# A decoder trunk on one NeuronCore: another order of the chunk steps in the token mixer

## What is computed

```
m = w_out( [retention heads | HGRN2 heads | sliding-window attention] (x @ w_in) )
x = layernorm(alpha * x + m)
x = layernorm(alpha * x + w_down(relu(w_up(x))^2))
```

## Time and profile before

| | |
|---|---|
| median of 3 runs | 2735.28 us (2732.26 to 2736.43) |
| the profiled execution, its own time | 2732.12 us |
| its span, first to last instruction | 2730.3 us |
| TensorE busy | 2555.8 us, 94% of the span |
| VectorE, GpSimd, ScalarE busy | 1680.6, 997.7 and 836.7 us |
| mean granted TensorE clock | 0.973 |

### The profile page before, as it was taken

The page is one execution under the profiler, slowest core; times in us unless marked ns, Lnnn a source line. Parts: engine busy times, 40 slices in busy tenths (PEclk is TensorE's granted clock), DMA queues, the critical chain, the costliest instruction groups (busy, mean ns, idle before and its releaser), DMA issues. The chain is left out here.

```text
span 2730.3 us, 45275 instructions
## 1 busy us (share of the span) xinstructions
PE 2555.8 (94%) x18126; PEld 2366.2 (87%) x18126; DVE 1680.6 (62%) x3361; ACT 836.7 (31%) x1667; POOL 997.7 (37%) x1052
## 2 busy tenths in 40 slices
PE   7999988789999999999899999887999999999996
PEld 7998866588999999999899987666989999999996
DVE  3136678558855666666851367884596555666668
ACT  3235665232322221111122455661322222111110
POOL 0027666531555531122000466664325555222220
PEclk9999999789999999999999999997999999999998
DMA  4442232162233253223343531321622233432323
GB/s 168 148 157 88 90 108 54 34 197 82 80 108 113 95 181 94 92 93 95 109 146 130 166 105 57 106 69 40 196 76 95 95 123 116 158 95 91 94 79 112
DMA packets 225889, 295.83 MB, mean 108 GB/s; under 512 B 28817, under 2 KB 177617, under 8 KB 225649
## 3 DMA queue, kind: packets, MB, share of 16 engines
q1 hardware_dynamic: 225680, 292.94, 33.5%
HBM read 217.27 MB, written 77.66 MB: 108 GB/s over the span
## 5 line engine op out<-in xcount | busy, mean ns | idle before, releaser
L1089 PE MATMUL ps<-hid_hi,wd_hi 128*128 128x256 f32 (+2 forms) x800 | 257.5, 322 | 12.7 <-DVE acc_b L2778 6.7
L1090 PE MATMUL ps<-hid_lo,wd_hi 128*128 128x256 f32 (+2 forms) x800 | 255.3, 319 | 0.0
L1089 PE MATMUL ps<-hid_hi,wdl_hi 128*128 128x256 f32 (+2 forms) x800 | 255.2, 319 | 0.0
L1090 PE MATMUL ps<-hid_lo,wdl_hi 128*128 128x256 f32 (+2 forms) x800 | 255.1, 319 | 0.0
L1091 PE MATMUL ps<-hid_hi,wd_lo 128*128 128x256 f32 (+2 forms) x800 | 255.1, 319 | 0.0
L1091 PE MATMUL ps<-hid_hi,wdl_lo 128*128 128x256 f32 (+2 forms) x800 | 254.8, 318 | 0.0
L2762 DVE TENSOR_TENSOR acc_a<-ps,acc_a 128x512 f32<-128x512 f32 x208 | 143.9, 692 | 152.3 <-PE ps L1091 152.3
L3077 POOL TENSOR_TENSOR wq_lo_S<-ws,wq_hi_S 128x512 fp32r<-128x512 f32 x104 | 199.1, 1923 | 104.3 <-ACT wq_hi_S L2087 104.3
L2762 DVE TENSOR_TENSOR acc_b<-ps,acc_b 128x256 f32<-128x256 f32 (+1 forms) x416 | 178.2, 439 | 74.2 <-PE ps L1091 69.2
L3055 POOL TENSOR_TENSOR wl_lo<-wl_raw,wl_hi 128x2048 fp32r<-128x2048 f32 x14 | 63.8, 4558 | 415.7 <-ACT wl_hi L1789 415.6
L1089 PE MATMUL ps<-wi_hi,u_hi 128*128 128x320 f32 x600 | 185.7, 309 | 2.1 <-DVE wi_lo L2273 2.1
(11 more groups left out here) (329 smaller groups left out, 7872.2 us busy)
## 6 DMA issues: line engine op xcount, KB each, us to landing
wd_raw<-in_w_down SPq DMA_DIRECT2D x32, 1024.0 KB, 4.9
wq_raw<-in_w_up SPq DMA_DIRECT2D x26, 1024.0 KB, 6.1
wl_raw<-in_w_in SPq DMA_DIRECT2D x20, 1024.0 KB, 5.1
wi_raw<-in_w_in SPq DMA_DIRECT2D x15, 1280.0 KB, 6.6
hidscr<-h SPq DMA_DIRECT2D x32, 544.0 KB, 7.9
out_y<-xn SPq DMA_DIRECT2D x32, 512.0 KB, 4.6
hidscr<-h SPq DMA_DIRECT2D x32, 512.0 KB, 7.1
hid_raw<-hidscr SPq DMA_DIRECT2D x32, 512.0 KB, 3.5
```

The costliest lines, as they stand in the source:

```text
L1089: nc.tensor.matmul(out, a_hi, b_hi, start=start, stop=False)
L1090: nc.tensor.matmul(out, a_hi, b_lo, start=False, stop=False)
```

## The change

No instruction of arithmetic is added or taken away. Five lists are put in another order.

1. ScalarE: `window_weights` is cut into `_a` and `_b`, and all of `gates_sigmoid(g)` stands between them. From step 4 on, `dense c` stands at the end of the step, behind `gates_log`, and in step 4 still ahead of `split_wo(l, 0)`.
2. TensorE: the gates' transposes stand between the transposes of waves A and B.
3. VectorE, `heads_merge`: `cat_h` ahead of the state updates. `gates_sigmoid` is cut after its clip, the rest is `gates_keys`, right behind it.
4. VectorE: `front_silu` moves from ahead of `front_levels` to behind `heads_rstd`; `heads_low` of a prompt chunk moves into the next step, behind `front_queries`.
5. GpSimd: the low parts of `OUT_AFTER` move from the end of a step to the next one, behind `values` and a wait for the next gates (`f1`).

```diff
@@ TensorE, mix_step
                         window_weights(f, h, "A")
-                        window_weights(f, h, "B")
                         if g:
                             gate_transposes(g, f, h)
+                        window_weights(f, h, "B")
@@ ScalarE
-                def window_weights(c):
+                def window_weights_a(c):
                     act.wait_ge(wpe.sem, wpe.at("TA", c.w))
                     copy(probT[:, 0]...).then_inc(wa.step("TA"), 1)
+
+                def window_weights_b(c):
                     act.wait_ge(wpe.sem, wpe.at("TB", c.w))
...
                         window_norm(f, "B")
-                        dense(step, "c")
-                        window_weights(f)
+                        if step < 4:
+                            dense(step, "c")
+                        window_weights_a(f)
                         if g:
                             gates_sigmoid(g)
+                        window_weights_b(f)
                         dense(step, "d")
...
                     if f and f.prompt and g:
                         gates_log(g)
+                    if f and f.prompt and step >= 4:
+                        dense(step, "c")
                     if step == 4:
                         split_wo(l, 0)
@@ VectorE, heads_merge
-                    if c.prompt:
-                        heads_states(c)
                     dve.wait_ge(md.sem, md.at("sr", c.n))
                     v.tensor_tensor(cat_h[0:rows, :], ...).then_inc(md.step("rh"), 1)
+                    if c.prompt:
+                        heads_states(c)
@@ VectorE, mix_step
+                    past = chunk_at(l, step - 2)
                     if f:
                         front_queries(f)
+                    if past:
+                        heads_low(past)
                     if h:
                         heads_keys(h)
...
                     if f:
-                        front_silu(f)
                         front_levels(f)
...
                     if h:
                         heads_rstd(h)
+                    if f:
+                        front_silu(f)
                     if f and f.prompt:
                         window_sums(f, "B")
...
                             gates_sigmoid(g)
+                            gates_keys(g)
                         window_low(f)
...
                     if h and not h.prompt:
                         decode_states_h(h)
-                    if h:
                         heads_low(h)
@@ GpSimd, mix_step
                     if f:
                         values(f, h)
+                    if step - 1 in OUT_AFTER:
+                        if f:
+                            pool.wait_ge(gc.sem, gc.at("f1", f.n))
+                        for out in OUT_AFTER[step - 1]:
+                            split_wo(l, out)
+                    if f:
...
                         gate_weights(f)
...
-                        for out in OUT_AFTER.get(step, ()):
-                            split_wo(l, out)
```

More of the change, by code:

```diff
@@ L2330, in gates_sigmoid, with gates_keys @@
                                     ALU.mult, ALU.min).then_inc(gc.step("clip"), 1)
+                def gates_keys(c):
+                    dve.wait_ge(gc.sem, gc.at("clip", c.n))
                     dve.wait_ge(gh.sem, gh.at("r", c.n))
@@ L2625, in mix @@
                 gates_sigmoid(chunk_at(l, 0))
+                gates_keys(chunk_at(l, 0))
                 v.memset(st_r[:], 0.0).then_inc(zd.step("r"), 1)
```

## The result

| | before | after |
|---|---|---|
| median of 4 runs | 2735.86 us (2732.26 to 2742.40) | 2777.69 us (2772.82 to 2783.93) |
| ratio, 95% interval | | 1.0143 (1.0122 to 1.0165) |
| span of the profiled execution | 2730.3 us | 2773.1 us |
| mean granted TensorE clock | 0.973 | 0.960 |

The account below looks back on a forecast made before the run. TensorE's work (2555.8 of 2730.3 us) plus its gaps was taken as the bound. Layer terms of 5.05 and 4.55 us gave 9.6, so 2732.1 became 2741.7 us, median 2744.9; range 2730 to 2751.

Parts of the forecast that it names:

- the change, which adds no work, can only move gaps: Whole kernel: time is TensorE's work, busy 2555.8 of 2730.3 us, plus gaps; only the gaps would change.
- `window_out` at TA+6.2: Steps 5 to 7: `window_out` starts 6.2 us after TA, the start of wave A's transposes, 1.35 us later than before.
- `window_low` follows `window_out` (1.95 us) and its high part (0.6 us): TA+8.85: Step 6: `window_low` starts 8.85 us after wave A's transposes start (TA), instead of 9.10; net -0.25 us.
- The wait that I named as a sign: Steps 5 to 7: TensorE's wait on ScalarE ahead of `window_out` would be near 2.5 us.
- the +0.2: Step lengths 5 to 6 and 6 to 7: each 0.2 us longer, bounds -1.2 to +0.9.
- The lock that the prediction weighed: VectorE's clip beside GpSimd's split: begun first, the clip would be free and each of two step lengths 0.6 us shorter.
- Step 1: 0, for `g_qe` is early and ScalarE then waits for a load of weights: Step 1 of the mixer: the reordered ScalarE copies cost 0 us.
- rival C: Late silu delays SyncE's `hb` loads and output weights queued behind; some 3 us more a layer, 2751 us; chance 0.12.
- Step 4 to 5: Late drains delay the first output weights, `s_kT` and `dense a1`: 3.35 us a layer, bounds 2.3 to 4.1.
- -0.25 and +0.2: Step 7 into 8: 0.25 us shorter; step 8: 0.2 us longer, silu standing ahead of the decode window on VectorE.
- A: Rival: late output weights cost little, 1 us at step 4 into 5; +5 us, 2740 us; chance 0.20.
- B: Rival, faster: VectorE's chain keeps its gains, 1.45 us off each of three lengths, steps 4 to 7; chance 0.16.

Follow-up runs that it names:

- Run 4: Changed kernel plus 20 throwaway identity transposes on TensorE ahead of `window_out` in each of the 8 prompt steps; ratio 1.0106 to the kernel before.
- run 6: Kernel before with ScalarE's gate functions between its copies of waves A and B, plus 16 throwaway TensorE transposes ahead of `window_out`; ratio 0.9999.
- run 12: Changed kernel, wave B copied first, `dense c` late only from step 5, silu late only in steps 4 to 7, GpSimd's split waiting for the clip; ratio 0.9943.
- run 9: Kernel before with only ScalarE's `dense c` of step 4 moved behind `gates_log`; ratio 1.0031.
- run 3: Changed kernel with `front_silu` put back ahead of `front_levels`; ratio 1.0089 to the kernel before.
- run 11: Changed kernel, but wave B copied before the gate functions, `dense c` late only from step 5, silu late only in steps 4 to 7; ratio 0.9949, 2724.53 us.
- run 5: Kernel before with only ScalarE's gate functions and the `g_q` copy put between its copies of waves A and B; ratio 1.0041.

## Why the size was wrong

The premise that failed first is "the change, which adds no work, can only move gaps": 24.6 of the 42.8 us are the same work, done at a lower clock. The sum moved rows and kept their durations, and had no term for the clock.

**`window_out` at TA+6.2: right place, wrong duration.** In the sum the step that failed is "`window_low` follows `window_out` (1.95 us) and its high part (0.6 us): TA+8.85". I moved `window_out` by 1.35 us and kept the duration of its row, 1.94 us. The wait that I named as a sign grew from 1.5 to 3.8 us (I had said 2.5; TensorE's last transposes also end at TA+2.5, not at TA+3.4 as before), and behind that wait the clock is at 1.2 GHz. Run 4 puts `window_low` back at TA+8.9 by nothing but work in the hole, and run 6 removes the whole price of the interleave. Over the 14 profiled executions, 224 prompt steps: with under 0.5 us of wait ahead, `window_out` was never slow (over 2 us) in 90; with 0.5 to 1.6 us in 4 of 73; with 1.6 to 2.6 us in 5 of 18; with more in 41 of 43. The Trainium skill has this, page "TensorE: Matmul & The Clock Gate", section "HAM oscillation — how this bites in real kernels": waits between bursts put TensorE back to the low clock, so that each next burst starts cold. The runs agree: in steps 5 to 7 of the changed kernel `window_out` takes 3.10 to 3.61 us for 1.94. I had not weighed the rule. The trace of before has one such place, in layer 1, of which I made nothing:

```profile
1793.16 1.78 PE L1085 MATMUL ps<-ident,prob 128*128 128x128 f32 x8 [0.51 <-ACT prob L1900]
...
1796.45 3.68 PE L1427 MATMUL ps<-probT,s_v 128*64 128x512 f32 x8 [0.65 <-ACT probT L1908]
```

The transposes ahead of it, 1.78 us for 1.09, are slow already, behind waits of 1.26 and 0.51 us; so the one wait next to an instruction does not decide alone.

**Steps 5 to 7, the +0.2.** Without the clock they are 35.5 to 35.9 us (run 4): +0.5 to +0.9, at the upper bound. That the clip is held by GpSimd's split was right (2.42 us for the first of its two). The lock that the prediction weighed (the Trainium skill, page "SBUF — State Buffer", section "SBUF: two separate sides": whoever starts first keeps it for the whole instruction) agrees with run 12: with the clip ahead of the split it takes 0.48 us. The length 6 to 7 falls by 1.0 us, where I had given 0.6; that of 5 to 6 does not clearly fall.

**Steps 1 to 3.** "Step 1: 0, for `g_qe` is early and ScalarE then waits for a load of weights" took that wait as cover. That is the other term that failed: the sum had 0.5 us for these four lengths, and 13.7 were measured. The wait was the next bound: the load itself landed later, behind loads of `hb` that the late silu lets out just ahead of it. Silu has a consumer besides the list it stands in, SyncE, and I saw that (rival C) but looked for its price only in the output weights. In all eight profiled executions with silu early in steps 0 to 3, that of before among them, ScalarE's waits in the four places sum to 2.9 to 6.4 us; in the six with it late, to 9.2 to 12.8. That the transfers share bandwidth was not tried by itself; shown is that the order of issue goes with it. The waits grew by 7.9 us in sum, the lengths by 13.7, and TensorE's work behind them ran at the low clock: with work in TensorE's other waits (run 4) 9.7 of the 13.7 us are gone, though ScalarE waits nearly as long. The same four lengths vary too: they sum to 162.0 to 168.5 us in the eight executions with silu early, and to 172.4 to 177.6 in the five others with it late.

**Step 4 to 5.** The mechanism and the chain were right. From the drains to the weights it took 6.0 us, where the sum had 6.3 from the rows. The 5.5 us estimated beside it rest on a section of the Trainium skill (page "DMA: Bandwidth & Descriptors") on DMAs that GpSimd issues; these are SyncE's. Alone it costs 2.9 us a layer (run 9), 3.35 in the sum. In the whole change it cost 4.5 and 5.4, above my bound of 4.1: `window_out` was slow as well, and TensorE's clock is 0.50 in 378.7 to 385.5 and in 389.0 to 395.8 us, behind its two waits (2.94 and 3.23 us). Run 4 left the length at 40.7 and 41.3, so most of the excess is not from the first of them.

**Steps 7 to 9.** I had -0.25 and +0.2. In layer 1, step 8 to 9 grew by 4.4 us. VectorE and GpSimd there:

```profile
1900.52 3.71 DVE L2560 TENSOR_SCALAR s_prob<-s_prob,rden 128x160 f32<-128x160 f32 x2
```
```profile
1900.91 2.34 POOL L3079 TENSOR_TENSOR wo_lo<-wo_in_lo,wo_hi 128x1024 fp32r<-128x1024 f32 x1
```

Silu ahead of the decode window moved `s_prob` (the decode tokens' window probabilities) by 1.5 us into the split of GpSimd; before, it took 1.01 us in this layer and ended ahead of the split. With silu early it took 1.33 (run 3) and 0.78 (run 11). But layer 0 of the kernel before has this meeting already:

```profile
512.03 3.24 DVE L2551 TENSOR_SCALAR s_prob<-s_prob,rden 128x160 f32<-128x160 f32 x2
```
```profile
511.74 2.34 POOL L3060 TENSOR_TENSOR wo_lo<-wo_in_lo,wo_hi 128x1024 fp32r<-128x1024 f32 x1
```

That goes with the two lengths of before, 41.8 in layer 0 and 37.1 in layer 1. Over the 14 profiled executions `s_prob` is held (2.8 us or more) in all 10 cases with silu late in step 8 and in 4 of the 18 with it early; the length 8 to 9 has a mean of 41.3 us where it is held and of 37.7 where it is not. Each of the two groups still varies by several us, and that stays open.

**The rivals.** A fell: the weights cost 2.9 us a layer alone. B fell for the change as a whole, but its mechanism, VectorE's chain keeping what it is given, is what runs 11 and 12 use. C was the nearest in kind, wrong in place.

## What to carry to other kernels

A wait that grows on TensorE has two prices: its length, and the work behind it at the low clock. The second can be the only one that counts: here the later end of a wait cost nothing by itself, the low clock behind it cost 11 us, and throwaway transposes in the wait took that back. When a producer is moved later, follow every consumer, the DMA queue too, and ask what its transfers will now be issued next to. And cut a change of many parts into them before judging it: without the interleave, and with two other edits kept only in the steps where they pay, the rest of this one makes the kernel 0.5% faster.

## What the hardware showed that I had not expected

- TensorE is busy 24.6 us longer over the same 18,126 matmuls; the granted clock in the wait of step 6 is still 1.00, and 0.51 in the work behind it, which takes 3.15 us for 1.94.
- `window_out` behind a wait of 3.10 us was slow in 7 of 8 steps (run 5); 1.97 us of added transposes in that wait kept it at 1.94 us in all 8 (run 6).
- A load of 1 MB of late weights landed in 4.8 to 6.5 us, in three places in about 7.0, when the loads of `hb` had gone long before, and in 6.0 to 8.1 us when they had been issued 2 to 4 us ahead of it.
- The same clip of 128 x 256 took 0.48 us for both instructions when free, 2.61 us begun 0.1 us after a GpSimd split.
- `s_prob` in the decode step took 0.78 to 1.33 us when it began clear of a GpSimd split and 2.8 to 3.7 us when it met one, as in one layer of the kernel before.
